# One of nine scoring stages moved five chunks earlier in a hybrid decoder trunk (one core of Trainium2)

## The chip, the cores and the metric

The kernel runs on one core of a Trainium2 chip. It is one launch. The metric is the device time of the whole program in microseconds. The engines are TensorE (PE, with its weight loads as PEld), VectorE (DVE), ScalarE (ACT), GpSimd (POOL) and SyncE (SP), which issues nearly all loads of weights.

## What is computed

A decoder trunk of two layers on 256 tokens of width 2048: an HGRN2 mixer and a conv-GLU, then a short convolution mixer and a conv-GLU, and a final norm. The change lies in the HGRN2 mixer alone. Cut to that:

```python
proj = xn @ w_in                                  # 2048 x 8192, float32
q, fr, v, g = split(proj, 4)
q = silu(q) * 128 ** -0.5
f = lb + (1 - lb) * sigmoid(fr);  k = 1 - f;  logf = log(f)
b = cumsum(logf)                                  # over time, per head
A = einsum('bhtd,bhsd,bhtsd->bhts', q, k, exp(b[t] - b[s]))    # s <= t
o = einsum('bhts,bhsv->bhtv', A, v) + ...         # state of earlier chunks
o = rms_norm(o, out_gain) * silu(g);  return o @ w_out
```

The diagonal of A (s = t) needs no decay: it is the sum over d of q times k of the same token.

## The kernel before

Each weight matrix comes in **chunks** of 512 KB (816 in all) through a ring of four slots. SP loads a chunk into `raw`; ACT copies it rounded to `w_parts[..., 0, :]` (the high part, `split` at L363 to L367); DVE subtracts to get the low part (`split` at L632 to L638). PE multiplies with both: the "highs" (L1185, or L1208 in the value group) and the "lows" (L1195 or L1216). ACT and DVE prepare chunk c+4 at the place of chunk c in their own order, and wait there until PE has used chunk c.

The first phase, `HGRN_IN`, is a loop of four iterations i, each with four heads. An iteration has four groups g of eight chunks: forget gate (g=0), query (g=1), value (g=2, "V group") and output gate (g=3, "gate group"). The places of the two last are counted together as n, so that n = 0 to 7 is the value group and n = 8 to 15 the gate group. Every engine has its own program with the same loops; in each, work of the recurrence stands at chosen n.

PE works on pairs of chunks. In the gate group the order is highs of both, the stage behind the first, lows of both, the stage behind the second. In the value group it is: highs of both for token block 0, lows of both for block 0, then for block 1 highs and lows of the first, its stage, highs and lows of the second, its stage.

**Stages.** The scores A are built in nine stages for each iteration, in two halves of a PSUM tile `side` that take turns. `PLAN` holds (chunk n behind which PE runs the stage, kind, level m). Levels 0 to 7 are blocks of the triangle of A; level -1 is the diagonal. For stages of level 1 and up DVE makes the operands `ql` and `kl` two chunks ahead (`level_operands`, L850) and updates `fpre` one chunk ahead (`prefixes`, L882); PE multiplies (L1378); one chunk behind, DVE moves the result into `a_diag` (`take_stage`, L890; L903, or L897 for the diagonal). A stage on PE waits until the one before the last has been taken (`stage_free`, L1157).

**The diagonal (level -1)** has no operands but a product: DVE writes `tb = qh * kh` at the end of place `OWN_PRODUCT` (L992), ACT writes its high part into `own_parts` at the beginning of place `OWN_HIGH` (L516), DVE its low part at the beginning of place `OWN_LOW` (L879), and PE sums both over the partitions with a matrix of ones (four 512-wide matmuls, L1372).

**The accumulator.** `acc` has two sets. Each part of a group begins in one, and PE may begin only when enough earlier ones have been emptied (`acc_free`, L1303). In the value group both sets hold values, one per block of 128 tokens, and it is ACT that empties them, by `values(i, 0, ...)` and `values(i, 1, ...)` (L376 to L383), both in the place of chunk n = 7. The gate group's first part (n = 8 to 11) takes set 0 and its second (n = 12 to 15) set 1.

ACT's program in `HGRN_IN`, at each place n, in this order (L389 to L402, `ahead` is `gates_and_products`, L504):

```python
if ahead:
    ahead(i, g, kk)                      # L391: OWN_HIGH stands here
c = phase.c0 + g * phase.cpg + kk
if ends and g == phase.wide_group:       # n = 7
    values(i, 0, c)                      # L395
if not last:
    split(i, phase, c + RING)            # L397
if ends and g == phase.wide_group:
    values(i, 1, c)                      # L399
```

and what stands in `ahead` for the diagonal is:

```python
if n == OWN_HIGH:
    act_e.wait_ge(product_ready, at(i, 2, 2))
    nc.scalar.activation(own_parts[:, 0], tb[:]..., ACT.Copy)
```

DVE's place n has `levels` first (L994 to L1022), then the low part of chunk n+4 (L620), then the combination of an accumulator set if a part ends there (L622), then `hgrn` (L960 to L992, the product at its end).

Of the kernel before, what the change touches and what calls it, by code (L numbers as in the profile page):

```python
# [57 lines left out]
class Phase:  # L58
# [31 lines left out]
    def runs(self, first, g, end):  # L90
# [4 lines left out]


V_GROUP = 2
PAIR_SPLIT, OWN_PRODUCT, OWN_HIGH, OWN_LOW = 1, 9, 10, 12
HGRN_IN = Phase(None, 4, 4, DT, scales=3, wide_group=V_GROUP)
HGRN_OUT = Phase(HGRN_IN, 2, 2, DT)  # L100
UP0 = Phase(HGRN_OUT, 11, 2, DT, scales=2)
# [18 lines left out]


LEVEL, OUTPUT = range(2)
PLAN = [(3, LEVEL, 0), (5, LEVEL, 1), (6, LEVEL, 2), (8, LEVEL, 3), (10, LEVEL, 4),
        (12, LEVEL, 5), (13, LEVEL, 6), (14, LEVEL, -1), (15, LEVEL, 7), (17, OUTPUT, 0)]
LEAD = 2
HGRN_STAGES = len(PLAN)
RS_AT = 6
# [22 lines left out]
def trunk(nc, x, parameters, hgrn_w_in, hgrn_w_out, sc_w_in, sc_w_out, ffn_w_up, ffn_w_down, final_norm, identity,  # L150
          level_masks, out):
    with ExitStack() as ctx:
# [436 lines left out]
        def _(dve):  # L589
# [286 lines left out]
            def product_low_parts(i, n, product, parts):  # L876

                dve.wait_ge(product_hi_ready, at(i, 2, n + 1))
                v.tensor_tensor(parts[:, 1], product.rearrange("p j t -> p (j t)"), parts[:, 0].bitcast(F32),  # L879
                                ALU.subtract).then_inc(product_parts_ready, 1)  # L880

            def prefixes(i, m):  # L882

                n = LEVELS[m]
                pre = halves(fpre[:], n)
                shape = [P, TG * T // (2 * n), n]
                await_mark(i)
                mark(v.tensor_tensor(pre[:, :, 1], pre[:, :, 1], pre[:, :, 0, n - 1:n].to_broadcast(shape), ALU.mult))  # L888

            def take_stage(i, stage):  # L890

                s = S_HGRN + stage
                _, _, m = PLAN[stage]
                src = side[:, s % STAGES]
# [59 lines left out]
            def last_take(i, g, kk):  # L954

                for stage, (after, what, _) in enumerate(PLAN):
                    if what == LEVEL and g * HGRN_IN.cpg + kk - 2 * HGRN_IN.cpg == after + 2:
# [36 lines left out]
            def levels(i, first, g, kk):  # L994
# [14 lines left out]
                if n == OWN_LOW:  # L1009
                    product_low_parts(i, 1, tb[:], own_parts)  # L1010
                done = [stage for stage, (after, what, _) in enumerate(PLAN) if what == LEVEL and n == after + 1]
                for stage in done:
                    dve.wait_ge(stage_done, at(i, HGRN_STAGES, S_HGRN + stage + 1))
                    v.sem_inc(stage_seen, 1)
                for after, what, m in PLAN:
                    if what == LEVEL and 0 <= m < len(LEVELS) - 1 and n == (after - LEAD + 1 if m else 1):
                        prefixes(i, m)
                for after, what, m in PLAN:
                    if what == LEVEL and m > 0 and n == after - LEAD:
# [425 lines left out]
```

## Time and profile before

| | |
|---|---|
| time, median of 3 runs | 2335.78 us (2335.21 to 2336.14) |
| time of the profiled execution | 2335.99 us |
| its span, first to last instruction | 2334.2 us |
| PE busy | 2320.7 us (99%) |
| DVE busy | 1694.3 us (73%) |
| ACT busy | 1054.0 us (45%) |
| granted clock, mean | 0.999 |

The time of an execution is 1.8 us more than its span. The four iterations of `HGRN_IN` end about 409 us after the start; the change touches nothing behind that.

### The profile page before, as it was taken

How to read it: one execution, taken by the hardware profiler on the slowest of the kernel's cores; microseconds unless marked ns; L12 is line 12 of the kernel's file. 1: busy time of each engine (PE TensorE's matmuls, PEld its weight loads, DVE VectorE, ACT ScalarE, POOL GpSimd, SP SyncE). 2: the span in 40 equal slices, each digit the busy share in tenths (PEclk: the TensorE clock that was granted, in tenths of full speed). 3: DMA queues.
4: the chain of work that ended last, by engine and by line, in shares of the span. 5: the costliest groups of instructions: out<-in, count | busy, mean ns of one | idle time of the engine just before them, and what ended most of it. 6: DMA issues, size and time to landing. Idle time of an engine off the chain costs nothing.

```text
span 2334.2 us, 36359 instructions
## 1 busy us (share of the span) xinstructions
PE 2320.7 (99%) x12692; PEld 2021.1 (87%) x12692; DVE 1694.3 (73%) x2127; ACT 1054.0 (45%) x1157; POOL 2.8 (0%) x9
## 2 busy tenths in 40 slices
PE   9999999999999999999999999999999999999998
PEld 8888888888888888888888888888888888888887
DVE  7978879868788788765556676766788788785544
ACT  7444444554444444434444444444444444443443
POOL 0000000000000000000000000000000000000000
PEclk9999999999999999999999999999999999999999
DMA  7555555565656656565565656665655656665664
GB/s 245 163 177 158 176 167 162 169 199 181 195 181 190 190 183 194 187 198 191 190 191 184 192 185 193 184 195 174 199 182 186 197 180 191 194 204 185 192 192 158
DMA packets 380297, 434.88 MB, mean 186 GB/s; under 512 B 13360, under 2 KB 325040, under 8 KB 380080
## 3 DMA queue, kind: packets, MB, share of 16 engines
q1 hardware_dynamic: 379200, 431.26, 59.3%
q10 hardware_dynamic: 1008, 2.43, 0.3%
q8 instruction: 56, 0.92, 0.2%
q14 instruction: 33, 0.27, 0.0%
HBM read 431.54 MB, written 2.10 MB: 186 GB/s over the span
## 4 chain that ended last, share of the span: by engine, by line
PE 93%; DVE 3%; issue 2%; DMA 1%; ACT 1%; SPq 0%; DVEq 0%; ACTq 0%
PE acc L1185 45%; PE acc L1195 24%; PE acc L1251 7%; PE acc L1252 7%; PE acc L1253 7%; PE acc L1208 2%; PE acc L1216 1%; DVE w_parts L637 1%; DMA raw<-in_hgrn_w_in 1%; PE side L1378 0%; PE side L1355 0%; DVE fpre L888 0%; DVE a_diag L903 0%; DMA h<-in_x 0%; ACT w_parts L367 0%
## 5 line engine op out<-in xcount | busy, mean ns | idle before, releaser
L637 DVE TENSOR_TENSOR w_parts<-raw,w_parts 128x1024 fp32r<-128x1024 f32 x816 | 983.6, 1223 | 573.1 <-PE acc L1195 297.8
L367 ACT ACTIVATE w_parts<-raw 128x1024 fp32r<-128x1024 f32 x815 | 856.4, 1058 | 943.8 <-PE acc L1185 617.4
L1185 PE MATMUL acc<-xn,w_parts 128*128 128x512 f32 x4352 | 1040.3, 391 | 1.1 <-DVE ta L664 0.6
L1185 PEld LDWEIGHTS acc<-xn,w_parts 128*128 128x128 f32 x4352 | 799.7, 188 | 156.9 <-DVE xn L688 1.2
L1195 PEld LDWEIGHTS acc<-xn,w_parts 128*128 128x128 f32 x4352 | 557.4, 191 | 20.7 <-DVE w_parts L637 0.4
L1195 PE MATMUL acc<-xn,w_parts 128*128 128x256 f32 x4352 | 566.9, 283 | 0.0
L1251 PE MATMUL acc<-w_parts,act 128*128 128x512 f32 x704 | 274.5, 390 | 0.0
L1253 PE MATMUL acc<-w_parts,act 128*128 128x512 f32 x704 | 274.0, 389 | 0.0
L1252 PE MATMUL acc<-w_parts,act 128*128 128x512 f32 x704 | 273.9, 389 | 0.0
L1253 PEld LDWEIGHTS acc<-w_parts,act 128*128 128x128 f32 x704 | 132.2, 188 | 27.7
L1251 PEld LDWEIGHTS acc<-w_parts,act 128*128 128x128 f32 x704 | 132.2, 188 | 27.1
L1252 PEld LDWEIGHTS acc<-w_parts,act 128*128 128x128 f32 x704 | 132.2, 188 | 26.9
L374 ACT ACTIVATE corr<-acc 128x512 f32<-128x512 f32 x144 | 85.7, 595 | 102.5 <-PE acc L1195 102.5
L1185 PE MATMUL acc<-act,w_parts 128*128 128x512 f32 x512 | 122.7, 391 | 0.0
L1185 PEld LDWEIGHTS acc<-act,w_parts 128*128 128x128 f32 x512 | 94.1, 188 | 18.2
L712 DVE SCALAR_TENSOR_TENSOR tb<-pad,par,tb 128x256 f32<-128x256 f32 x208 | 90.9, 481 | 12.2 <-DVE tb L710 0.3
L712 DVE SCALAR_TENSOR_TENSOR ta<-pad,par,ta 128x256 f32<-128x256 f32 x176 | 77.5, 482 | 11.9
L1195 PEld LDWEIGHTS acc<-act,w_parts 128*128 128x128 f32 x512 | 65.8, 191 | 2.6
L1195 PE MATMUL acc<-act,w_parts 128*128 128x256 f32 x512 | 66.6, 283 | 0.0
L664 DVE TENSOR_TENSOR pad<-acc,corr 128x512 f32<-128x512 f32 x96 | 65.5, 683 | 0.0
L450 ACT ACTIVATE ta<-ta 128x1024 f32<-128x1024 f32 x22 | 23.4, 1063 | 82.6 <-DVE ta L712 82.6
L673 DVE TENSOR_TENSOR pad<-pad,rs 128x1024 f32<-128x1024 f32 x48 | 58.9, 1226 | 1.7
(135 smaller groups left out, 903.5 us busy)
## 6 DMA issues: line engine op xcount, KB each, us to landing
raw<-in_ffn_w_up SPq DMA_DIRECT2D x352, 512.0 KB, 3.6
raw<-in_ffn_w_down SPq DMA_DIRECT2D x176, 512.0 KB, 4.4
raw<-in_hgrn_w_in SPq DMA_DIRECT2D x127, 512.0 KB, 3.8
raw<-in_sc_w_in SPq DMA_DIRECT2D x96, 512.0 KB, 4.7
raw<-in_hgrn_w_out SPq DMA_DIRECT2D x32, 512.0 KB, 3.5
raw<-in_sc_w_out SPq DMA_DIRECT2D x32, 512.0 KB, 4.7
h<-in_x SPq DMA_DIRECT2D x3, 512.0 KB, 8.7
final_w<-in_final_norm ACTq DMA_DIRECT2D x1, 1024.0 KB, 7.2
```

What stands on the lines that cost most here:

```text
L367: nc.scalar.activation(w_parts[:, c % RING, :, 0, :], raw[:, c % RING], ACT.Copy).then_inc(hi_ready, 1)
L374: nc.scalar.activation(corr[:], acc[:, a % SETS, :, T:], ACT.Copy).then_inc(corr_ready, 1)
L637: v.tensor_tensor(w_parts[:, c % RING, :, 1, :], raw[:, c % RING], w_parts[:, c % RING, :, 0, :].bitcast(F32), ALU.subtract).then_inc(lo_r ...
L664: v.tensor_tensor(dst[:, part * TW:(part + 1) * TW, :], acc[:, a % SETS, :, 0:T], corr[:], ALU.add) \
L673: v.tensor_tensor(dst, dst, rs[:, None, 0:T].to_broadcast([P, TG, T]), ALU.mult) \
L712: o = v.scalar_tensor_tensor(out=dst[:, j, :], in0=src, scalar=w, in1=dst[:, j, :], op0=ALU.mult, op1=ALU.add)
L1185: o = mm(to[:, j, :], w[:, q, 0, j * P:(j + 1) * P], src[:, k * KW + q, :, :].rearrange("p n t -> p (n t)"), start=begin and q == 0, stop= ...
L1195: o = mm(to[:, j, T:], w[:, q, 1, j * P:(j + 1) * P], src[:, k * KW + q, 0, :], start=False, stop=end and q == KW - 1, skip_group_check=True)
L1208: o = mm(acc[:, b, 0, :], x_block(src, k * KC + q, n, b), w[:, 2 * q:2 * q + 2, 0, :], start=begin and q == 0 and n == 0, stop=False)
L1251: mm(bank, x_hi, hi, start=begin and q == 0, stop=False)
L1252: low = mm(bank, x_hi, lo, start=False, stop=False)
L1253: high = mm(bank, x_lo, hi, start=False, stop=end and q == KC - 1)
```

## The change

The diagonal's product moves on DVE from the end of place 9 to the end of place 6, its high part on ACT from place 10 to the beginning of place 7, its low part on DVE from place 12 to place 8, and its stage on PE from behind chunk 14 to behind chunk 9, that is between the stages of levels 3 and 4. DVE takes it at place 10 instead of place 15. Since `PLAN` is a list in the order of the stages, the halves of `side` used by levels 4, 5 and 6 change places. No work is added or removed.

```diff
-PAIR_SPLIT, OWN_PRODUCT, OWN_HIGH, OWN_LOW = 1, 9, 10, 12
+PAIR_SPLIT, OWN_PRODUCT, OWN_HIGH, OWN_LOW = 1, 6, 7, 8
...
-PLAN = [(3, LEVEL, 0), (5, LEVEL, 1), (6, LEVEL, 2), (8, LEVEL, 3), (10, LEVEL, 4),
-        (12, LEVEL, 5), (13, LEVEL, 6), (14, LEVEL, -1), (15, LEVEL, 7), (17, OUTPUT, 0)]
+PLAN = [(3, LEVEL, 0), (5, LEVEL, 1), (6, LEVEL, 2), (8, LEVEL, 3), (9, LEVEL, -1), (10, LEVEL, 4),
+        (12, LEVEL, 5), (13, LEVEL, 6), (15, LEVEL, 7), (17, OUTPUT, 0)]
```

## Rows read from the trace of the kernel before

**Rows 1.** Waits from 20 to 400 us: engine and line, releaser, us, times, longest.

```profile
ACT act L516 <- DVE tb L992: 27.9, 4, 7.2
```

**Rows 2.** Busy us and instructions of PE, PEld, DVE, ACT, POOL in a stretch.

```profile
280.40:305.40 25.00, 24.18 (x146) 21.20 (x144) 24.79 (x35) 10.90 (x12) 0.00 (x0) 1.00 0.51 153
```

**Rows 3.** Timeline of PE, iteration 2: start us, us, instruction, idle before and releaser.

```profile
280.50 3.79 PE L1185 MATMUL acc<-xn,w_parts 128*128 128x512 f32 x16
284.12 1.05 PE L1378 MATMUL side<-ql,kl 128*128 128x128 f32 x8
284.93 2.16 PE L1195 MATMUL acc<-xn,w_parts 128*128 128x256 f32 x16
286.93 3.82 PE L1185 MATMUL acc<-xn,w_parts 128*128 128x512 f32 x16
290.58 1.05 PE L1378 MATMUL side<-ql,kl 128*128 128x128 f32 x8
...
300.66 3.92 PE L1185 MATMUL acc<-xn,w_parts 128*128 128x512 f32 x16
305.41 1.20 PE L1372 MATMUL side<-act,sum_ones 128*128 128x512 f32 x4 [0.83 <-DVE a_diag L903]
306.44 2.07 PE L1195 MATMUL acc<-xn,w_parts 128*128 128x256 f32 x16
```

**Rows 4.** Timeline of ACT, iteration 2, places 6 and 7, then 10.

```profile
278.94 0.67 ACT L382 ACTIVATE vt<-acc,rs 128x512 f32<-128x512 f32 x1
...
292.30 1.06 ACT L516 ACTIVATE act<-tb 128x1024 fp32r<-128x1024 f32 x1 [6.92 <-DVE tb L992]
293.27 1.99 ACT L367 ACTIVATE w_parts<-raw 128x1024 fp32r<-128x1024 f32 x2
```

**Rows 5.** Timeline of DVE, iteration 2, places 6, 7, 9, 10, 13 and 15.

```profile
282.08 1.26 DVE L637 TENSOR_TENSOR w_parts<-raw,w_parts 128x1024 fp32r<-128x1024 f32 x1
283.26 0.68 DVE L888 TENSOR_TENSOR fpre<-fpre 128x512 f32<-128x512 f32 x1
...
284.45 1.22 DVE L637 TENSOR_TENSOR w_parts<-raw,w_parts 128x1024 fp32r<-128x1024 f32 x1
...
291.05 1.22 DVE L992 TENSOR_TENSOR tb<-qh,kh 128x1024 f32<-128x1024 f32 x1
292.19 0.68 DVE L864 TENSOR_TENSOR ql<-qh,fpre 128x512 f32<-128x512 f32 x1
...
304.63 0.72 DVE L903 COPY_PREDICATED a_diag<-masks,side 128x512 f32<-128x512 uint8 x1
...
308.81 1.31 DVE L897 COPY_PREDICATED a_diag<-masks,side 128x1024 f32<-128x1024 uint8 x1
```

**Rows 6.** Timeline of PE and DVE, iteration 0, the same places.

```profile
80.04 3.79 PE L1185 MATMUL acc<-xn,w_parts 128*128 128x512 f32 x16
...
83.10 0.67 DVE L888 TENSOR_TENSOR fpre<-fpre 128x512 f32<-128x512 f32 x1
...
100.20 3.92 PE L1185 MATMUL acc<-xn,w_parts 128*128 128x512 f32 x16
105.34 1.17 PE L1372 MATMUL side<-act,sum_ones 128*128 128x512 f32 x4 [1.22 <-DVE a_diag L903]
106.35 2.06 PE L1195 MATMUL acc<-xn,w_parts 128*128 128x256 f32 x16
```

**Rows 7.** Timeline of PE: the first and the last matmuls of the program.

```profile
1.08 6.20 PE L1341 MATMUL side<-ones 128*128 128x128 f32 x32 [1.08 <-POOL ones L353]
7.04 2.51 PE L1185 MATMUL acc<-xn,w_parts 128*128 128x512 f32 x8
...
2326.30 0.39 PE L1253 MATMUL acc<-w_parts,act 128*128 128x512 f32 x1
```

**Rows 8.** The same at the program's end; the column behind POOL's is the granted clock.

```profile
2330.00:2331.00 1.00, 0.00 (x0) 0.00 (x0) 0.00 (x0) 0.22 (x1) 0.00 (x0) 0.79 0.84 307
2331.00:2332.00 1.00, 0.00 (x0) 0.00 (x0) 0.00 (x0) 0.00 (x0) 0.00 (x0) 0.50 1.03 365
```

## The prediction

> **What bounds the kernel now.** I read the page first. PE is busy for 99% of the span, so a change can only matter by idle time that it adds to or takes from PE, or by PE's clock. The page counts averages, so I next asked for the waits around the four iterations of `HGRN_IN`. ACT stands idle for 27.9 us in four times, some 7 us in each iteration, before the diagonal's high part (L516), because DVE is late with the product [rows 1]. ACT's wait harms nobody today, since ACT works four chunks ahead and the accumulator's set that it empties next isn't wanted soon.
>
> The third view is the busy time by stretch. From 280.4 to 305.4 us, the gate group, DVE is busy 24.79 us of 25 [rows 2]: it works off a queue and is behind PE. PE misses 0.82 us of busy time in that stretch, all of it before the diagonal's stage (L1372), which waits for DVE to take an earlier stage [rows 3]. The last view is the timeline of the three engines; there I look at what stands in each queue ahead of and behind every instruction that moves. Iterations 1 and 3 show the same distances as iteration 2 within 0.05 us; in iteration 0 DVE is 0.3 us further behind when chunk 8 begins [rows 6].
>
> **What the change removes.** Behind chunk 14 there is no stage any more. In iteration 2 the highs of chunks 14 and 15 start at 300.66; sixteen of them take 3.65 us (286.93 to 290.58), so the stage could start at 304.31, and four matmuls of 512 columns take 0.91 us at that pace. The lows could then start at 305.22 and start at 306.44 [rows 3]: 1.22 us are lost there. By the same working iteration 0 loses 106.35 - (100.20 + 3.65 + 0.91) = 1.59 us [rows 6]. Four iterations: 1.59 + 3 x 1.22 = 5.25 us, all given back if nothing replaces it. The stage of level 7 behind chunk 15 comes in its place. It needs operands that DVE makes at place 13 and a half of `side` that is emptied at place 13, with the place-12 low part gone from the queue; I cost it at nothing.
>
> The matmuls, copies and subtractions themselves are as many as before and as long, so they are worth nothing. No DMA is moved.
>
> **What the change adds.** The high part moves on ACT from place 10 to the beginning of place 7, and there it stands ahead of `values(i, 0)`, the copy that empties accumulator set 0. PE's first matmul of chunk 8 needs `acc_free` at 8i + 7. The count starts at 2 and each earlier iteration adds 8; in this one groups 0 and 1 add four, so the fifth must be `values(i, 0)`. So PE's way now leads over: DVE's product at the end of place 6, ACT's high part, `values(i, 0)`, PE. Today that copy starts at 278.94 and ends 0.9 us before PE starts chunk 8 at 280.50 [rows 3, 4]. The cover is 0.9 us, and the product alone is later than that: DVE's own queue has place 6's low part at 282.08.
>
> Step by step in iteration 2. DVE is free for the product at 283.26, where the prefix of place 7 starts today [rows 5]; nothing ahead of it has changed. The product takes 1.22 us, ACT starts 0.03 us behind it (291.05 + 1.22 to 292.30), the next ACT instruction 0.97 us later (292.30 to 293.27), `values` takes 0.67 us [rows 4, 5], and PE starts 0.06 us behind what releases it (304.63 + 0.72 to 305.41) [rows 3, 5]. Sum 2.95 us, so PE starts chunk 8 at 286.21 instead of 280.50: 5.71 us late. The first matmuls behind a wait cost 0.12 us more (the four at 305.41 took 1.03 us to the next line instead of 0.91) [rows 3]. Together 5.83 us. In iteration 0: 83.10 + 2.95 - 80.04 + 0.12 = 6.13 us [rows 6]. Four iterations: 6.13 + 3 x 5.83 = 23.62 us. Nothing can absorb it, since PE has no other idle time to give.
>
> **What is late next.** Behind the waiting instruction on ACT are `values(i, 0)`, the high part of chunk 11 and `values(i, 1)`. The second values are wanted at chunk 12 and the high part by PE after chunks 8 and 9, both some 6 us later. But DVE's low part at place 7 needs that high part: it is ready at about 283.26 + 1.22 + 0.03 + 0.97 + 0.67 + 1.06 = 287.2, where DVE would come to it at 284.45 + 1.14 = 285.6 [rows 5], so DVE waits 1.6 us. DVE's queue thus falls back, to the level 4 stage, by the product (1.14, 291.05 to 292.19), this wait (1.6), the low part (1.14 as well) and the taking (1.31 [rows 5]): 5.2 us, while PE was set back by 5.83 us. None of the other stages waited before, so none does now; and the diagonal's stage itself has its low part by about 289.7 and is reached at 286.3 + 3.62 + 0.81 + 2.0 = 292.8 [rows 3]. I cost second waits at nothing; the bounds are 0 and 1 us for each iteration, the size of today's.
>
> **The sum without the clock:** 23.62 - 5.25 = 18.4 us, or 2335.99 + 18.4 = 2354.4 us against the profiled execution. That execution stands 0.2 us above the median of the three runs.
>
> **The clock.** The new idle time is long enough to ask whether PE comes back at full clock. The last matmul of the program ends at 2326.69; the granted clock means 0.79 in the microsecond from 2330 and is 0.50 from 2331 on [rows 7, 8], which is 1.2 GHz of 2.4. A mean of 0.79 between 1.00 and 0.50 puts the fall at 2330.58, 3.9 us after the last matmul. The new gap is 5.6 to 6.0 us, 1.7 to 2.1 us more. What a return costs is bounded by the start of the program: 32 small matmuls take 5.96 us there (1.08 to 7.04), while eight of the same width take 0.81 us in mid-run (284.12 to 284.93), so 32 would take 3.2 [rows 3, 7]. A start from rest lost some 2.7 us. Below, the cost is nothing, if the clock holds. One fall in the trace doesn't show whether it always comes at the same distance. I take half of 4 x 2.7 = 10.8 us, 5 us in all, and keep 0 and 10.8 for the range.
>
> The Trainium skill, page "TensorE: Matmul & The Clock Gate", Part 1, says that the throttled clock is the default, that activity releases it, and that it also depends on when a gap falls by a clock of the chip's own. By that rule some of the four gaps would halve the clock and others not, which would give a time between the two ends. The fall in the last microseconds agrees with the first half of it; that it differs from gap to gap no row here shows.
>
> **The rivals.** *A: the clock holds in all four gaps.* Against it speaks that the gaps are longer than 3.9 us; for it, that they are so by 2 us only. Time 2354.4 us. *B: it falls in all four and the full price is paid each time.* For it the same row; against it, that the start is the coldest case. Time 2354.4 + 10.8 = 2365.2 us. *C, the other side: ACT's values are not held up,* because DVE has the product before PE has finished chunk 7. Then only the 5.25 us go and the time is 2330.7 us. It decides if product and high part end by 279.5; DVE's queue shows the product's place at 283.26, so this needs DVE to be 6 us earlier than in any of four iterations. Almost nothing speaks for it, apart from a misreading of the order of ACT's queue or of the count of `acc_free`. *D: second waits in the gate group,* on DVE being late for the stages behind 12 and 13; up to 1 us each time, 2354.4 + 4 + 5 = 2363 us.
>
> **How the numbers follow.** The likeliest case is the stall with the clock falling in part of the gaps or for part of the price: chance 0.54, 2354.4 + 5 = 2359.4 us, its own range 2356 to 2363. A has 0.25, B 0.1, C 0.03, D 0.08. The range takes in A with 2 us for what the chain of spacings may be off (0.5 us in each iteration), and B with the same: 2352.5 to 2367. A measurement of this kernel tells 0.2%, 4.7 us, from no change. Only C would come out faster (0.02), or with a partly shorter stall within 4.7 us (0.02); all others are slower (0.96).
>
> **What would show it.** The profile after should have a wait of PE at L1185 of 5.5 to 6 us four times, released by ACT's `vt` copy (L382); the product (L992) starting right behind place 6's low part at about 283 us less or plus the shift of earlier iterations; L516 directly behind it, and L382 directly behind that. The wait before L1372 should be gone. The iterations should be 104.5 us apart or more instead of 100. The granted clock in the 4 us behind each gap tells the likeliest case from A. It would be wrong if PE starts chunk 8 without waiting, if the waits are 3 us or less, or if a wait for DVE turns up behind chunks 10 to 15.

## The result, and the profile after

| | before | after |
|---|---|---|
| time, median | 2335.77 us (2335.21 to 2336.14) | 2362.60 us (2362.13 to 2362.68) |
| profiled execution | 2335.99 us | 2362.61 us |
| its span | 2334.2 us | 2360.7 us |
| mean granted clock | 0.999 | 0.994 |

The change made the kernel slower by 26.8 us: the ratio is 1.0115, with a 95% interval from 1.0103 to 1.0127. The forecast was 2359.4 us, in a range of 2352.5 to 2367.

The waits of the kernel after, from 20 to 430 us, answer to [rows 1]:

```profile
...
PE acc L1185 <- ACT vt L382: 22.3, 4, 5.8
ACT act L516 <- DVE tb L992: 21.9, 4, 5.6
...
DVE w_parts L637 <- ACT w_parts L367: 16.6, 10, 2.1
```

The first of these lines is new, and the longest among PE's: PE waits four times for the copy of the values, and it no longer waits before L1372. ACT still stands idle before L516, as it did before, but now the value copy is queued behind it.

The timeline of PE in iteration 2 of the kernel after (this iteration lies 14 us later than before) answers to [rows 3]:

```profile
294.32 0.61 PE L1216 MATMUL acc<-w_parts,x_mirror 128*128 128x512 f32 x2
300.43 5.48 PE L1185 MATMUL acc<-xn,w_parts 128*128 128x512 f32 x16 [5.50 <-ACT vt L382]
305.75 1.05 PE L1378 MATMUL side<-ql,kl 128*128 128x128 f32 x8
306.56 2.16 PE L1195 MATMUL acc<-xn,w_parts 128*128 128x256 f32 x16
308.56 1.09 PE L1372 MATMUL side<-act,sum_ones 128*128 128x512 f32 x4
```

Chunk 8 could start 0.46 us behind 294.32, as it did before, and starts at 300.43: a gap of 5.65 us. Its sixteen matmuls then take 5.32 us to the next line, where they took 3.62 in [rows 3]. ACT and DVE in the same stretch, answering to [rows 4] and [rows 5]:

```profile
292.25 1.06 ACT L367 ACTIVATE w_parts<-raw 128x1024 fp32r<-128x1024 f32 x1 [3.93 <-PE acc L1208]
298.75 1.06 ACT L516 ACTIVATE act<-tb 128x1024 fp32r<-128x1024 f32 x1 [5.44 <-DVE tb L992]
299.71 0.67 ACT L382 ACTIVATE vt<-acc,rs 128x512 f32<-128x512 f32 x1
```

```profile
296.34 1.25 DVE L637 TENSOR_TENSOR w_parts<-raw,w_parts 128x1024 fp32r<-128x1024 f32 x1
297.50 1.21 DVE L992 TENSOR_TENSOR tb<-qh,kh 128x1024 f32<-128x1024 f32 x1
298.63 0.68 DVE L888 TENSOR_TENSOR fpre<-fpre 128x512 f32<-128x512 f32 x1
```

This is the chain link by link: product 297.50, high part 298.75, values 299.71, PE 300.43. From the product's start to PE it is 2.93 us, where the sum had 2.95.

The granted clock in the microseconds around that gap. The first busy time is PE's; the clock is the column behind POOL's, 1.00 at 2.4 GHz and 0.50 at 1.2 GHz:

```profile
296.00:297.00 1.00, 0.00 (x0) 0.00 (x0) 1.00 (x2) 0.00 (x0) 0.00 (x0) 0.97 0.93 316
297.00:298.00 1.00, 0.00 (x0) 0.00 (x0) 1.00 (x2) 0.00 (x0) 0.00 (x0) 0.50 0.24 83
...
303.00:304.00 1.00, 1.00 (x4) 0.77 (x4) 1.00 (x2) 0.00 (x0) 0.00 (x0) 0.62 0.08 18
304.00:305.00 1.00, 1.00 (x6) 0.82 (x5) 0.99 (x3) 0.90 (x1) 0.00 (x0) 1.00 0.73 187
```

The clock falls to half, 1.2 GHz, at about 296.9 us, 2.0 us after PE's last matmul, and returns at about 303.8. A mean between the two levels tells when within its microsecond the clock changed. The microseconds of fall and return in iterations 0, 1 and 3:

```profile
85.00:86.00 1.00, 0.00 (x0) 0.00 (x0) 0.76 (x2) 1.00 (x2) 0.00 (x0) 0.65 0.83 258
...
92.00:93.00 1.00, 1.00 (x7) 0.86 (x6) 0.00 (x0) 0.00 (x0) 0.00 (x0) 0.93 0.00 0
...
191.00:192.00 1.00, 0.00 (x0) 0.00 (x0) 1.00 (x2) 0.00 (x0) 0.00 (x0) 0.56 0.00 0
...
197.00:198.00 1.00, 1.00 (x4) 0.81 (x3) 1.00 (x4) 0.45 (x1) 0.00 (x0) 0.53 0.62 134
...
406.00:407.00 1.00, 0.27 (x1) 0.27 (x2) 0.23 (x1) 1.00 (x3) 0.00 (x0) 0.58 0.99 342
...
409.00:410.00 1.00, 1.00 (x5) 0.78 (x4) 1.00 (x2) 0.00 (x0) 0.00 (x0) 0.71 0.00 0
```

All four gaps look like this:

| iteration | gap of PE | clock falls after the last matmul | matmuls of chunks 8 and 9 | over 3.62 us |
|---|---|---|---|---|
| 0 | 5.90 us | 4.8 us | 6.49 us | 2.87 us |
| 1 | 5.67 us | 2.9 us | 5.73 us | 2.11 us |
| 2 | 5.65 us | 2.0 us | 5.32 us | 1.70 us |
| 3 | 5.67 us | 4.9 us | 5.09 us | 1.47 us |
| sum | 22.9 us | | | 8.15 us |

The last column follows from how long the clock stays low once PE is back. The clock returns 5.9, 4.2, 3.3 and 2.9 us behind the start of chunk 8 (92.1, 197.9, 303.8 and 409.6 us against 86.26, 193.73, 300.43 and 406.73). Half of each is 2.9, 2.1, 1.7 and 1.4 us. Part of the 8.15 us would be there at full clock too: behind the same gaps with the clock held at 1.00 (the filled kernel below) the sixteen matmuls take 3.76 to 3.79 us instead of 3.62, since the first ones behind a wait are slower (the restart). That is 0.6 us in all. So the fall of the clock by itself costs 7.5 us.

The wait behind chunk 14 was 4.8 us in the four iterations rather than 5.25 (worked out below). 22.9 + 8.15 - 4.8 = 26.2 us of the 26.6 that lie between the two profiled executions. Of the other 0.4 us, 0.3 are there before chunk 8 of iteration 0 (80.36 instead of 80.04 us).

### The profile page after: what moved, and what is told of

The parts are those of the page before. It is cut to its first block, busy times and chain, and to the rows that moved or that the text cites. A ratio compares the mean times of both kernels' runs of the same rounds, so it can differ in the third digit from the quotient of the medians.

```text
span 2360.7 us, 36361 instructions
## 1 busy us (share of the span) xinstructions
PE 2328.3 (99%) x12692; PEld 2027.2 (86%) x12692; DVE 1695.4 (72%) x2127; ACT 1054.9 (45%) x1157; POOL 2.8 (0%) x9
## 4 chain that ended last, share of the span: by engine, by line
PE 93%; DVE 4%; issue 2%; DMA 1%; ACT 1%; DVEq 0%; SPq 0%; ACTq 0%
PE acc L1185 47%; PE acc L1195 24%; PE acc L1253 7%; PE acc L1251 7%; PE acc L1252 7%; DVE w_parts L637 1%; PE side L1378 1%; DMA raw<-in_hgrn_w_in 1%; PE side L1355 0%; DVE a_diag L903 0%; DVE kl L870 0%; DVE fpre L888 0%; PE side L1163 0%; DVE ql L864 0%; DVE ta L673 0%
## 5 line engine op out<-in xcount | busy, mean ns | idle before, releaser
L1185 PE MATMUL acc<-xn,w_parts 128*128 128x512 f32 x4352 | 1048.1, 393 | 23.2 <-ACT vt L382 22.3
L1185 PEld LDWEIGHTS acc<-xn,w_parts 128*128 128x128 f32 x4352 | 805.3, 190 | 182.3 <-ACT vt L382 23.9
L1185 PE MATMUL acc<-act,w_parts 128*128 128x512 f32 x512 | 122.7, 391 | 0.0
L1185 PEld LDWEIGHTS acc<-act,w_parts 128*128 128x128 f32 x512 | 94.1, 188 | 18.2
```

The source lines that it names most:

```text
L1185: o = mm(to[:, j, :], w[:, q, 0, j * P:(j + 1) * P], src[:, k * KW + q, :, :].rearrange("p n t -> p (n t)"), start=begin and q == 0, stop= ...
```

## The experiments

Every kernel is compared with the kernel before on the same chip. The median of before lay between 2335.44 and 2335.63 us. Where a kernel adds lines, the numbers of the lines behind them are higher by as many (L1186 is L1185, L1382 is L1378).

### Values first: only ACT's order is undone

```diff
-                            if ahead:
-                                ahead(i, g, kk)
                             c = phase.c0 + g * phase.cpg + kk
+                            if ends and g == phase.wide_group:
+                                values(i, 0, c)
+                            if ahead:
+                                ahead(i, g, kk)
                             last = isinstance(i, int) and i * phase.cpi + c + RING >= CHUNKS
-                            if ends and g == phase.wide_group:
-                                values(i, 0, c)
```

> The changed kernel, but ACT empties set 0 of the accumulator before it takes the diagonal's high part; both stay at place 7. Theory (the copy values(i, 0) is held up because it is queued behind the high part): PE starts chunk 8 without a wait, the 22.9 us of gaps and the 8.2 us at half clock go. What is left is that the diagonal's low part comes late: DVE's place 7 must wait for the high part of chunk 11 until about 286.5 us in iteration 2, its low part ends at about 288.9, and the stage behind chunk 9 could start at 286.9, so PE waits some 2.1 us there, four times. 2336.0 - 5.25 + 4 x 2.2 = 2339.6 us. Rival (ACT as a whole is late there, wherever the copy stands): the waits at chunk 8 stay and the time is near 2362.

Measured: 2344.33 us, ratio 1.0038 (1.0025 to 1.0050). The four waits at chunk 8 are gone, so the rival falls. The remaining wait is where the theory put it and as long; iteration 2 on PE:

```profile
284.76 3.79 PE L1185 MATMUL acc<-xn,w_parts 128*128 128x512 f32 x16
...
293.30 1.19 PE L1372 MATMUL side<-act,sum_ones 128*128 128x512 f32 x4 [1.95 <-DVE act L879]
294.33 3.80 PE L1185 MATMUL acc<-xn,w_parts 128*128 128x512 f32 x16
```

But the time is 4.7 us above the expectation. Iteration 1 shows where that is: the same gap, and slow matmuls behind it.

```profile
190.57 2.04 PE L1372 MATMUL side<-act,sum_ones 128*128 128x512 f32 x4 [1.94 <-DVE act L879]
192.41 4.57 PE L1185 MATMUL acc<-xn,w_parts 128*128 128x512 f32 x16
196.81 1.05 PE L1378 MATMUL side<-ql,kl 128*128 128x128 f32 x8
```

```profile
190.00:191.00 1.00, 0.43 (x1) 0.44 (x2) 1.00 (x3) 0.51 (x1) 0.00 (x0) 0.81 0.36 79
191.00:192.00 1.00, 1.00 (x4) 0.71 (x4) 0.97 (x4) 0.00 (x0) 0.00 (x0) 0.50 0.91 246
```

PE starts at 190.57 and the clock falls at about 190.6, although the gap was only 2 us. The four matmuls of the stage and the sixteen behind them take 6.24 us to the next line, instead of 4.67 in iteration 2. The clock falls in iterations 0, 1 and 3, not in 2; in iterations 0 and 3 it does so 0.4 and 1.0 us after PE has come back, at 87.84 and 394.44:

```profile
88.00:89.00 1.00, 1.00 (x4) 0.77 (x5) 1.00 (x3) 0.00 (x0) 0.00 (x0) 0.61 0.78 212
...
395.00:396.00 1.00, 1.00 (x5) 0.78 (x4) 0.97 (x3) 0.00 (x0) 0.00 (x0) 0.71 0.94 296
```

The kernel with its gap filled, below, tests this.

### High part at place 8

`OWN_HIGH` is 8 instead of 7, nothing else.

> The changed kernel with the diagonal's high part on ACT at place 8 instead of 7, so behind both value copies and the high part of chunk 11. Theory: no wait at chunk 8, full clock; DVE's place 7 isn't held up, the low part ends at about 288.0 in iteration 2, so PE waits some 1.1 us before the diagonal's stage behind chunk 9: 2336.0 - 5.25 + 4 x 1.2 = 2335.5 us, within 0.1% of the kernel before. Rival (the new place of stage and taking costs by itself): clearly above 2340.

Measured: 2335.82 us, ratio 1.0001 (0.9992 to 1.0011). One number moved by one undoes the whole loss. PE in iteration 2, and the low part that it waits for:

```profile
287.90 1.19 PE L1372 MATMUL side<-act,sum_ones 128*128 128x512 f32 x4 [0.99 <-DVE act L879]
```

```profile
286.55 1.22 DVE L879 TENSOR_TENSOR act<-tb,act 128x1024 fp32r<-128x1024 f32 x1
```

The stage's new place trades the 1.2 us wait behind chunk 14 for one of 1.1 us behind chunk 9, and costs nothing by itself.

### The stage stays: only product and high part are moved, in the kernel before

```diff
-PAIR_SPLIT, OWN_PRODUCT, OWN_HIGH, OWN_LOW = 1, 9, 10, 12
+PAIR_SPLIT, OWN_PRODUCT, OWN_HIGH, OWN_LOW = 1, 6, 7, 12
```

> The kernel before with only the product (place 6) and its high part (place 7) moved; the low part stays at place 12 and the stage behind chunk 14. Theory (product and high part alone cause the loss): four waits of 5.6 to 5.9 us at chunk 8 with the clock at half behind them, and no wait before the stage behind chunk 14, since PE is set back by more than DVE lacks there: 2360 to 2364 us. Rival (the stage's new place costs): 2336 us or a little less.

Measured: 2362.19 us, ratio 1.0116 (1.0099 to 1.0133), the same as the whole change. PE in iteration 2:

```profile
297.75 6.74 PE L1185 MATMUL acc<-xn,w_parts 128*128 128x512 f32 x16 [5.51 <-ACT vt L382]
...
324.61 1.07 PE L1372 MATMUL side<-act,sum_ones 128*128 128x512 f32 x4
```

The gap is there and the wait behind chunk 14 is not: a PE set back by more than 5.6 us has given DVE the time that it lacked. So the 4.8 us that the change gives back (5.25 in the forecast) would have been given back by the gap alone.

### The gap filled: what the clock costs

This stands in PE's program of the changed kernel, at the end of chunk 7. The results of the matmuls are never used.

```diff
+FILL = 16
...
+                if n == 7:
+                    pe.wait_ge(stage_free, at(i, HGRN_STAGES, S_HGRN + 3 + 1))
+                    for _ in range(FILL):
+                        mm(side[:, (S_HGRN + 3) % STAGES, 0:P], ones[:], ones[:], start=True, stop=True)
```

> The changed kernel with 16 matmuls of ones by ones (3.2 us of work for PE, results never used) issued at the end of chunk 7 as soon as a half of side is free, so inside the gap before chunk 8. The gap to chunk 8's matmuls stays as long. Theory (8.2 us of the loss are matmuls at 1.2 GHz behind an idle PE): the granted clock stays 1.00 or falls only for a shorter time, and the time comes to 2354.4 us, up to 2357 if it falls in one gap. Rival (the excess over the sum is another wait): it stays at 2362 to 2363. A third: the 16 matmuls themselves set PE back, then the time goes up by as much as they reach beyond the gap.

Measured: 2354.33 us, ratio 1.0081 (1.0064 to 1.0098). The stretches of 15 us around its four gaps, and then those around the gaps of the kernel after, which come up to 7 us later:

```profile
79.00:94.00 15.00, 13.04 (x84) 11.38 (x83) 12.90 (x18) 5.28 (x6) 0.00 (x0) 1.00 0.40 124
184.00:199.00 15.00, 13.34 (x86) 11.64 (x85) 12.90 (x18) 5.28 (x6) 0.00 (x0) 1.00 0.40 126
289.00:304.00 15.00, 13.34 (x86) 11.66 (x85) 12.93 (x17) 5.28 (x6) 0.00 (x0) 1.00 0.39 119
394.00:409.00 15.00, 13.34 (x86) 11.83 (x85) 12.96 (x16) 5.28 (x6) 0.00 (x0) 1.00 0.43 126
```

```profile
80.00:95.00 15.00, 9.25 (x39) 7.43 (x38) 10.19 (x15) 5.27 (x6) 0.00 (x0) 0.77 0.39 118
187.00:202.00 15.00, 9.50 (x44) 7.78 (x43) 10.95 (x16) 5.28 (x6) 0.00 (x0) 0.77 0.42 133
...
400.00:415.00 15.00, 9.50 (x48) 7.89 (x47) 11.58 (x16) 5.28 (x6) 0.00 (x0) 0.89 0.42 131
```

The clock stays at 1.00, and 8.3 us are gone. What is left, 2354.3, is close to the sum of the prediction without the clock (2354.4). Between the two profiled executions it is 8.4 us (2362.61 and 2354.20), and 0.9 us of these lie ahead of the first gap: chunk 8 of iteration 0 could start at 79.48 here and at 80.36 in the kernel after. That leaves 7.5 us for the clock, as above. Iteration 2 shows that chunk 8 is still late, at 294.95. The filling isn't what holds it: PE starts 0.05 us behind the end of ACT's copy.

```profile
291.11 3.84 PE L1368 MATMUL side<-ones 128*128 128x128 f32 x32 [1.66 <-DVE a_diag L904]
294.95 3.92 PE L1186 MATMUL acc<-xn,w_parts 128*128 128x512 f32 x16
```

```profile
294.23 0.67 ACT L383 ACTIVATE vt<-acc,rs 128x512 f32<-128x512 f32 x1
```

### Values first, with its gap filled

The same filling, with 8 matmuls, before the stage behind chunk 9 of the kernel with the values first.

> The kernel with the values first (2344.3 us, where 2339.6 was expected), with 8 matmuls of ones by ones (1.6 us) put into its 2.0 us gap before the diagonal's stage. Theory (the 4.7 us that it was over its expectation are matmuls at 1.2 GHz behind gaps of only 2.0 us): the clock stays at 1.00 and the time comes to 2339.6 us. Rival (another wait made them): 2344.3 us.

Measured: 2339.55 us, ratio 1.0017 (1.0007 to 1.0027). The filling took away 4.8 us, so the 4.7 us were the clock, behind gaps of 2 us.

### Product one place earlier

`OWN_PRODUCT` is 5 instead of 6 in the changed kernel.

> The changed kernel with DVE's product at place 5 instead of 6, the high part still ahead of the value copy at place 7. Theory (the gap before chunk 8 ends 2.95 us behind the moment at which DVE is free for the product, whatever else): the product starts at about 278.97 us of iteration 2, PE's gap is 1.4 us instead of 5.7 (1.7 in iteration 0), and no wait comes behind it. 2336.0 + 1.84 + 3 x 1.54 - 5.25 = 2337.2 us with the clock at 1.00, and 1.5 to 2 us more for each gap behind which it falls (three of the four 2.0 us gaps of the kernel with the values first had it), at most 2344. Rival (ACT's lateness has another cause): gaps of more than 3 us, above 2350.

Measured: 2337.39 us, ratio 1.0008 (0.9999 to 1.0017). DVE and PE in iteration 2:

```profile
280.75 1.22 DVE L992 TENSOR_TENSOR tb<-qh,kh 128x1024 f32<-128x1024 f32 x1
```

```profile
283.69 3.94 PE L1185 MATMUL acc<-xn,w_parts 128*128 128x512 f32 x16 [1.26 <-ACT vt L382]
```

The product's start to PE is 2.94 us again. The gaps are 1.4 us (1.7 in iteration 0): they shrink by what the product moves. No microsecond around them has a clock below 1.00.

### ACT's copy doubled

```diff
+                    nc.scalar.activation(ta[:], tb[:], ACT.Copy)
                     nc.scalar.activation(own_parts[:, 0], tb[:]..., ACT.Copy)
```

> The changed kernel with a second copy of the product on ACT (to a tile that nobody reads then), directly ahead of the high part at place 7. Theory (ACT's copy is one link of the chain to PE's chunk 8): each gap grows by the spacing of one such copy, 0.97 us, to 6.6 us, and no other wait appears: 4 x 0.97 = 3.9 us more than the changed kernel, 2366.5 us; the price of the clock stays what it is or goes up or down by 3 us at most, as the gaps' ends shift: 2363.5 to 2369.5. Rival (DVE, not ACT's queue, sets when PE starts): 2362.6 us.

Measured: 2365.77 us, ratio 1.0129 (1.0113 to 1.0146), 3.2 us above the changed kernel. The waits of PE for L382 sum to 26.1 us instead of 22.3, so 3.8 us more, as expected. The matmuls behind the gaps take 8.2 us over 3.62 each, as before. The total rises by 0.6 us less than the waits because this profiled execution ends chunk 7 of iteration 0 0.7 us sooner (its last line starts at 79.24, not at 79.90), ahead of everything that the copy touches.

```profile
301.83 6.33 PE L1186 MATMUL acc<-xn,w_parts 128*128 128x512 f32 x16 [6.44 <-ACT vt L382]
```

### The kernel before, taking first

```diff
+                for stage in done:
+                    take_stage(i, stage)
                 for after, what, m in PLAN: ... prefixes(i, m)
                 for after, what, m in PLAN: ... level_operands(i, m)
-                for stage in done:
-                    take_stage(i, stage)
```

> The kernel before, with the diagonal behind chunk 14 as it was, but at every place DVE takes the finished stage before it makes the next prefix and operands, not behind them. Theory (PE's 1.2 to 1.6 us wait behind chunk 14 is for the taking of level 5, which stands behind 1.2 us of operands for level 7 that are wanted 4 us later): the taking ends at 304.1 instead of 305.4 us, PE waits 0 to 0.3 us, and no other stage becomes late: 2330.7 to 2331.5 us, 0.2% under the kernel before. Rival (DVE's queue as a whole is too long there and the wait only moves to another stage): 2335 to 2336 us.

Measured: 2331.36 us, ratio 0.9981 (0.9972 to 0.9990): 4.3 us less than before, and the fastest of all. In iteration 2 DVE has the taking ahead of the operands, and PE reaches L1372 3.76 us behind the start of the highs, without a wait:

```profile
301.18 0.73 DVE L903 COPY_PREDICATED a_diag<-masks,side 128x512 f32<-128x512 uint8 x1
301.80 0.67 DVE L864 TENSOR_TENSOR ql<-qh,fpre 128x512 f32<-128x512 f32 x1
```

```profile
298.36 3.92 PE L1185 MATMUL acc<-xn,w_parts 128*128 128x512 f32 x16
302.12 1.09 PE L1372 MATMUL side<-act,sum_ones 128*128 128x512 f32 x4
```

### Early diagonal with all three orders mended

`OWN_HIGH` = `OWN_LOW` = 8, the stage behind chunk 10 ahead of level 4's, and the first taking ahead of prefix and operands.

> The changed kernel with high part and low part both at place 8, the diagonal's stage behind chunk 10 ahead of level 4's, and the taking ahead of prefix and operands at every place (the second of two takings stays behind them). Theory (an early diagonal costs nothing once nothing stands ahead of the value copy and its low part has one more pair of chunks): the low part ends 2.8 us before the stage; small waits of 0.1 to 0.2 us for the taking of levels 3 and 4; 2331 to 2333 us, clock at 1.00. Rival (moving the diagonal ahead of four stages pushes DVE too far back in the gate group): waits of 1 us or more behind chunks 10 to 13, 2335 us or more.

Measured: 2334.22 us, ratio 0.9994 (0.9985 to 1.0003), between the two theories. Waits for the taking of levels 3 and 4 are there, as expected, but longer; both stages in iteration 2, by the weight loads:

```profile
290.53 0.97 PEld L1382 LDWEIGHTS side<-ql,kl 128*128 128x128 f32 x8 [0.56 <-DVE a_diag L903]
...
300.18 0.97 PEld L1382 LDWEIGHTS side<-ql,kl 128*128 128x128 f32 x8 [0.33 <-DVE a_diag L903]
```

These are the stages of levels 4 and 6. Each wait costs some 0.3 us of PE and 0.1 us for the restart, and there are two in each of four iterations: 3.2 us as an estimate. The kernel that only takes first, with the diagonal left behind chunk 14, is 2.9 us faster. An early diagonal puts some 3.6 us of DVE work (product, low part and its own taking) into the queue ahead of the taking of level 4, the first two of them ahead of that of level 3. There is a second reason for the wait at level 4: with the diagonal between them, its stage needs the half of `side` that level 3 used, where before it needed that of level 2, emptied earlier. No run separates the two.

## Why the prediction was right, and where it was off

**The new wait.** This was right in place, order and size. Gaps of 5.90, 5.67, 5.65 and 5.67 us stand against 6.01 and three times 5.71. The order of ACT's queue makes them, with a product that comes late. With the values first, or the high part one place later, they vanish; with the product one place earlier they shrink with it, and with a second copy they grow.

**The wait removed.** It went, and its size was put 0.4 us too high in all. The highs of chunks 14 and 15, which stand behind a stage, take 3.76 us where nothing waits (298.36 to 302.12 in the kernel that takes first), not the 3.65 of the pair in [rows 3] that stands behind lows. So the waits were 1.11 us and, in iteration 0, 1.48 us: 4.8 us. The new place of the stage is only one of the ways to lose this wait: the kernel in which the stage stays lost it as well. What decides is what DVE does before it takes level 5: with that taking first, the wait is gone and the diagonal where it was.

**No second waits.** This was right: the list of PE's waits has none behind chunk 8, and 2354.33 us with the gap filled against 2354.4 for the sum without the clock leaves little room for any. The wait of DVE at place 7 was 1.4 us (1.6 in the forecast). Rival D is out. So is C: chunk 8 waited in all four iterations.

**The clock.** This is the mis-sized term. The step was half of 4 x 2.7 = 10.8 us, "5 us in all". It measured 7.5 us, or 8.15 us with the 0.6 us of restart at full clock, for which the sum without the clock had 0.5. The clock fell behind all four gaps, and the matmuls behind them were 1.5 to 2.9 us too slow. The 3.2 us between forecast and time come together so: 2.7 us from the clock and the restart, 0.4 from the wait removed, 0.4 that no term had, and 0.3 less from the gaps. Rival A is out, since the clock fell. B had the number of falls right and the price of three of them too high. The 5 us were a middle between two bounds, and no row gave it. The time lies at the edge of the likeliest case's own range (2356 to 2363): the bounds held, the middle did not. What sets the price is how far the low stretch reaches behind PE's return, and that can't be told from the length of the gap: three gaps of 5.7 us cost 2.1, 1.7 and 1.5 us. Nor did the one fall in the trace of before, 3.9 us after the last matmul, give a distance to compare a gap with. The four measured distances are 2.0 to 4.9 us. The rule of the Trainium skill that the prediction weighed ("TensorE: Matmul & The Clock Gate", Part 1: what the clock does depends also on when the gap falls) agrees with that spread, and with the kernel with the values first, in which three of four gaps of 2.0 us had the clock fall.

## What to carry to other kernels

When a step is moved to a new place in an engine's queue, look first at what stands right behind that place and who waits for it: here a wait for the busiest engine was put ahead of a copy with 0.9 us of cover. Before moving work to cure a wait of the bounding engine, look at the order within the place where the late engine stands: taking a result before making operands that are wanted 4 us later gave 0.2%, and the move gave nothing even with the high part one place later (2335.82 us against 2335.44). A gap of the tensor engine has to be priced with the matmuls behind it: here 22.9 us of gaps cost 8.15 us more in that way.

## What the runs showed of the hardware that was not expected

The granted clock can halve behind an idle time of PE of only 2.0 us: it did in three of four such gaps of the kernel with the values first, 0.05, 0.4 and 1.0 us after PE had come back. In the kernel after it fell in one gap 2.0 us after the last matmul and in another only after 4.9 us, though the gaps were alike. With gaps of 1.7 us and less (the kernel with the product at place 5, and the kernel before) it held in all of them. Matmuls whose results nobody uses, issued into the gap, held it at 1.00. They were worth 8.3 us between the medians (7.5 by the working above), and 4.8 us in the kernel with gaps of 2.0 us.
